# Hybrid trunk on one core: token-tile scalar multiplications on GpSimd, low parts of the output weights on VectorE, and no branch at a layer's end

## What is computed

```python
for l in range(DEPTH):                                   # DEPTH = 2, SEQ = 512, D_MODEL = 1024
    sh_m, sc_m, g_m, sh_f, sc_f, g_f = split(c_act @ ada_w[l] + ada_b[l], 6)
    hm = rms_norm(x, norm_mix_g[l]) * (1.0 + sc_m) + sh_m
    z, xbc, dt_raw, cq, ckv, krope, mq, mk, mv = split(hm @ w_in[l])
    y_ssd = ssd_mixer(z, xbc, dt_raw, ...)
    y_mla = rms_norm(mla_mixer(cq, ckv, krope, ...), mla_out_g[l])
    y_moba = rms_norm(moba_mixer(mq, mk, mv, ..., rel_bias), moba_out_g[l])
    y = concatenate([y_ssd, y_mla, y_moba]) @ w_out[l]
    x = x + g_m * y
    hf = rms_norm(x, norm_ffn_g[l]) * (1.0 + sc_f) + sh_f
    x = x + g_f * moe_ffn(hf, ...)                       # top 2 of 16 experts, one group
```

## Time and profile before

| | before |
|---|---|
| median of 3 executions | 1483.41 us (1477.52 to 1484.29) |
| the profiled execution | 1484.28 us, its span 1482.5 us |
| mean granted TensorE clock | 0.949 of full speed |
| PE busy | 1331.1 us, 90% of the span |
| DVE busy | 1165.1 us, 79% |
| ACT busy | 735.0 us, 50% |
| POOL busy | 257.7 us, 17%, in 300 instructions |

### The profile page before, as it was taken

One profiled execution on the slowest core, in us unless ns is written; L12 is line 12 of the kernel. 1 busy time (PEld: TensorE's weight loads), 2 busy tenths in 40 slices (PEclk: granted clock), 3 DMA queues, 4 the chain that ended last, 5 costly groups with the idle time before them and its releaser, 6 DMA issues. The chain is left out here.

```text
span 1482.5 us, 17406 instructions
## 1 busy us (share of the span) xinstructions
PE 1331.1 (90%) x6467; PEld 1050.8 (71%) x6467; DVE 1165.1 (79%) x1372; ACT 735.0 (50%) x967; POOL 257.7 (17%) x300
## 2 busy tenths in 40 slices
PE   6799987869989999999949998886898999999994
PEld 3677865657878888888647777564677788888882
DVE  3669856894679999999855987398657899999985
ACT  1334343562337777777413342345413777777760
POOL 0100135461011000000120012339001110010002
PEclk9899997989999999999969999898899999999997
DMA  9676521423579999998548573133327899999955
GB/s 361 234 263 225 191 92 56 142 88 141 211 285 365 413 401 416 410 407 351 210 164 301 172 256 118 57 114 114 128 99 284 336 399 410 404 415 403 410 186 185
DMA packets 95461, 378.64 MB, mean 255 GB/s; under 512 B 5961, under 2 KB 8759, under 8 KB 85768
## 3 DMA queue, kind: packets, MB, share of 16 engines
q1 hardware_dynamic: 71816, 307.83, 54.7%
q0 software_dynamic: 15232, 55.63, 9.6%
q10 hardware_dynamic: 8320, 13.96, 2.7%
HBM read 344.58 MB, written 32.82 MB: 255 GB/s over the span
## 5 line engine op out<-in xcount | busy, mean ns | idle before, releaser
L1278 PE MATMUL ps<-mod_rounded,work_rounded 128*128 128x512 f32 x340 | 136.9, 403 | 1.1 <-DVE work_rounded L2284 1.1
L1280 PE MATMUL ps<-mod_rounded,work_rounded 128*128 128x512 f32 x340 | 134.6, 396 | 0.0
L1739 DVE SCALAR_TENSOR_TENSOR gain<-ring,csil,gain 128x512 f32<-128x512 f32 x134 | 111.6, 833 | 3.3
L1279 PE MATMUL ps<-ring_rounded,work_rounded 128*128 128x512 f32 x288 | 113.9, 396 | 0.0
L2143 DVE TENSOR_TENSOR ring_rounded<-ring,mod_rounded 128x2048 fp32r<-128x2048 f32 (+1 forms) x54 | 102.9, 1930 | 1.4
L1279 PE MATMUL ps<-work_rounded 128*128 128x512 f32 x256 | 101.0, 395 | 0.0
L2143 DVE TENSOR_TENSOR work_rounded<-work,mod_rounded 128x2048 fp32r<-128x2048 f32 (+1 forms) x48 | 91.3, 1931 | 9.9 <-ACT mod_rounded L1638 8.7
L2527 POOL DMA_INDIRECT work<-ffn_rows,slot_idx x34 | 42.0, 1236 | 302.8 <-PE ps L1264 270.1
L929 PE MATMUL ps<-ring_rounded,actT_rounded 128*128 128x512 f32 (+1 forms) x256 | 93.9, 367 | 0.0
L1638 ACT ACTIVATE mod_rounded<-ring 128x2048 fp32r<-128x2048 f32 (+1 forms) x54 | 85.9, 1625 | 0.0
L929 PE MATMUL ps<-work_rounded,mod_rounded 128*128 128x512 f32 (+1 forms) x192 | 77.1, 401 | 4.0 <-ACT work L1405 4.0
(11 more groups left out here) (371 smaller groups left out, 3647.2 us busy)
## 6 DMA issues: line engine op xcount, KB each, us to landing
ring<-in_ada_w SPq DMA_DIRECT2D x38, 1024.0 KB, 5.3
ring<-in_moe_w_gate SPq DMA_DIRECT2D x18, 2048.0 KB, 10.0
ring<-in_moe_w_up SPq DMA_DIRECT2D x18, 2048.0 KB, 10.4
ring<-in_moe_w_down SPq DMA_DIRECT2D x18, 2048.0 KB
work<-in_moe_w_up SPq DMA_DIRECT2D x16, 2048.0 KB, 10.7
work<-in_moe_w_down SPq DMA_DIRECT2D x16, 2048.0 KB, 11.6
work<-in_moe_w_gate SPq DMA_DIRECT2D x16, 2048.0 KB, 10.2
expert_rows<-work POOLq DMA_DIRECT2D x32, 512.0 KB, 7.9
```

What stands on the lines that cost most here:

```text
L1278: pe.matmul(ps[j][:, :], xl, hi, start=k == 0, stop=False)
L1279: pe.matmul(ps[j][:, :], xh, lo, start=False, stop=False)
L1280: mm = pe.matmul(ps[j][:, :], xh, hi, start=False, stop=k == KD - 1)
L1739: add(v.scalar_tensor_tensor(acc, w, csil[:, k:k + 1], acc, ALU.mult, ALU.add))
```

## The change

Four edits:

1. `times_rstd` on GpSimd is a loop over the four token tiles, each a `tensor_scalar` by the column of 1/rms, where it was one `tensor_tensor` with the column broadcast.
2. GpSimd no longer makes low parts of the output weights. VectorE makes (0, 1) at n = 25 and (1, 0) right before its wait on `yrs`. PE counts one semaphore instead of two.
3. The Ifs on `L < DEPTH - 1` are gone, so each layer, the last too, loads, rounds and subtracts for a next one.
4. PE's eight `by_token` products and VectorE's eight adds stand behind the Ifs on `nov > 1` instead of ahead of them (with the bodies rewritten to match).

```diff
@@ sync
-                with sp.If(L < DEPTH - 1):
-                    load_first_in(sp, (L + 1) % DEPTH)
-                    sp.dma_start(mod[:, 0:2 * D], mod_rows[bass.ds(L + 1, 1), 0:2 * D].broadcast_to([P, 2 * D])
-                                 ).then_inc(next_b, 16)
-                    sp.wait_ge(y_ps, 2 * (NTL - 1))
-                    load_mix_gain(sp, (L + 1) % DEPTH)
-                    sp.wait_ge(next_b, 16)
+                load_first_in(sp, (L + 1) % DEPTH)
+                sp.dma_start(mod[:, 0:2 * D], mod_rows[bass.ds(L + 1, 1), 0:2 * D].broadcast_to([P, 2 * D])
+                             ).then_inc(next_b, 16)
+                sp.wait_ge(y_ps, 2 * (NTL - 1))
+                load_mix_gain(sp, (L + 1) % DEPTH)
+                sp.wait_ge(next_b, 16)
@@ tensor, out_products
-                            pe.wait_ge(*OUT_LOW[2 * b + k // 4])
+                            pe.wait_ge(out_w_lo, 2 * b + k // 4 + 1)
@@ scalar
-                with a.If(L < DEPTH - 1):
-                    a.wait_ge(y_ps, 2 * (NTL - 1))
-                    first_in_hi(a)
+                a.wait_ge(y_ps, 2 * (NTL - 1))
+                first_in_hi(a)
@@ vector
-                    if n == 19:
-                        out_weights_lo(0, 0)
+                    if n in (19, 25):
+                        out_weights_lo(0, (n - 19) // 6)
...
                 for q in range(8 * T - 3 - FIRST_Y, Y_EARLY):
                     y_low(q)
+                out_weights_lo(1, 0)
                 v.wait_ge(yrs, 3)
...
-                with v.If(L < DEPTH - 1):
-                    last_out(True)
-                with v.If(L > DEPTH - 2):
-                    last_out(False)
+                e = NTL - 1
+                first_in_lo(v, 0, 2 * (len(IN_ORDER) - 1))
+                y_out(e, e % 2, halves=(0,))
+                first_in_lo(v, 1, 2 * (len(IN_ORDER) - 1))
+                y_out(e, e % 2, halves=(1,))
+                v.wait_ge(next_b, 16)
+                mix_gain(v)
@@ gpsimd
                 def times_rstd(dst, src, rstd_, n):
-                    return g.tensor_tensor(dst, src, rstd_.to_broadcast([P, T, n]), ALU.mult)
+                    for t in range(T):
+                        ins = g.tensor_scalar(dst[:, t, :], src[:, t, :], rstd_[:, t, :], None, ALU.mult)
+                    return ins
...
-                for b, half in ((0, 1), (1, 0)):
-                    g.wait_ge(out_w_hi, 2 * b + half + 1)
-                    raw, lo, hi = out_part(b, half)
-                    g.tensor_tensor(lo, raw, hi.bitcast(F32), ALU.subtract).then_inc(out_w_lo_g, 1)
```

More of the change, by code:

```diff
@@ L409, in trunk @@
     out_w_lo = sem("w_out_low_done")
-    out_w_lo_g = sem("w_out_low_done_by_gpsimd")
     hf_wr = sem("ffn_rows_stored")
@@ L1189, in _ @@
                 pv(8 * T - 1)
-                OUT_LOW = [(out_w_lo, 1), (out_w_lo_g, 1), (out_w_lo_g, 2), (out_w_lo, 2)]
                 def out_products(b, t, ks, opens=False, closes=False):
@@ L1330, in by_token @@
                                      start=True, stop=True)
[L1332 to L1335, removed]
                 with pe.If(nov > 1):
+                    pe.wait_ge(y_ev, 2 * NTL)
                     with pe.Fori(0, NOV - 1) as i:
                         with pe.If(nov > i + 1):
+                            for b in range(2):
+                                for t in range(T):
+                                    by_token(b, t).then_inc(cb_ps, 1)
                             pe.wait_ge(ov_x, i + 1)
@@ L1365, in _ @@
                             pe.wait_ge(ov_ye, i + 1)
-                            for b in range(2):
-                                for t in range(T):
-                                    by_token(b, t).then_inc(cb_ps, 1)
+                for b in range(2):
+                    pe.wait_ge(y_ev, 2 * (NTL - 1) + b + 1)
+                    for t in range(T):
+                        by_token(b, t).then_inc(cb_ps, 1)
             @block.scalar
@@ L2327, in add_by_token @@
                     return v.scalar_tensor_tensor(x_, ps[2 * t + b][:, :], over_w[:, t, n:n + 1], x_, ALU.mult, ALU.add)
[L2329 to L2344, removed]
                 hidden(NTL - 1)
@@ L2359, in _ @@
                         with v.If(nov > n):
+                            for b in range(2):
+                                for t in range(T):
+                                    v.wait_ge(cb_ps, 2 * T * (n - 1) + T * b + t + 1)
+                                    ins = add_by_token(n - 1, b, t)
+                            ins.then_inc(ov_x, 1)
                             v.wait_ge(ov_si, n)
@@ L2363, in _ @@
                             slot_tokens(n)
+                            v.wait_ge(ov_x, n)
+                            v.tensor_copy(over_w[:, :, 0:1], over_w[:, :, n:n + 1])
                             v.wait_ge(ov_yp, n)
@@ L2366, in _ @@
                             v.tensor_tensor(ysb[:, 0, 512:1024], ps[7][:, :], gf[:, 512:1024], ALU.mult).then_inc(ov_ye, 1)
[L2367 to L2371, removed]
+                            v.wait_ge(cb_ps, 2 * T * (n + 1))
+                for b in range(2):
+                    for t in range(T):
+                        v.wait_ge(cb_ps, T * b + t + 1)
+                        add_by_token(0, b, t)
             @block.gpsimd
```

## The result

The changed kernel takes 1516.06 us in the median of 4 executions (1515.55 to 1517.7), the kernel before 1483.85 (1477.52 to 1485.46) beside it: a ratio of 1.0226, 95% interval 1.0202 to 1.0250. It is slower. The forecast was 1512 us, range 1482 to 1530. The profiled execution has a span of 1513.9 us at a mean granted clock of 0.933, where before had 1482.5 and 0.949.

A forecast was written before the change was run, and what follows sets the result against it. PE, busy 90%, was taken to wait in attention for GpSimd's staging and a held VectorE instruction. From 1484.3, staging +35.8, low parts -11.0 and layer end +4.05 gave 1513.1, less 0.9 for the median: 1512 us, range 1482 to 1530.

The forecast's parts named there:

- Staging, +35.8: GpSimd's 20 staging instructions per layer become 80; longer stages that PE waits for add 17.9 us per layer, 35.8 in all.
- most of 0.924 is fixed: GpSimd's scalar multiply, 0.924 us for 128x256, is mostly fixed cost, so 32, 64, 96 elements take 0.57, 0.62, 0.67.
- each microsecond moves the rest by one: In five or six of eight staging stages, each microsecond of longer staging moves the rest of the layer.
- rival B: Dearer staging (+46) and PE's clock falling after longer waits, 4 to 8 us: 1527 to 1531 us, chance 0.15.
- the slack of the first stage: First head's staging has about 1.7 us to spare, so of 3.5 us growth only 1.8 reaches the path.
- 4.5 against 4.0 of slack: Fifth staging stage grows 4.5 us against 4.0 to spare, PE starting later, so it adds 0.
- The low parts, -11.0: VectorE's held instructions run normally, -15.6 us; its added subtractions cost 4.6 in all; net -11.0.
- the wait of 2.95: VectorE's 2.95 us wait at 339.69 for a GpSimd chain, expected to hide the half (1, 0) subtraction at no cost.
- Rival C: Low parts give nothing back, since VectorE's chain after step 25 stays as long: 1524 us, chance 0.10.
- The layer's end, +4.05: Without the branch, the last layer's end, last store to GpSimd's drain end, takes 24.15 us like layer 0, not 20.1.
- The branches and moved order, 0: Dropped branches, and PE's eight products and VectorE's eight adds moved across an If, cost nothing beside other work.
- Rival A: Small scalar staging instructions are cheap, below about 0.40 us for 128x64, so not slower: 1481 us, chance 0.17.

## Why the prediction was right, and where it was not

The time (1512 against 1516.06) and the direction were right, and the mechanism too: the small instructions lengthen stages that PE waits for. That it came so near is partly luck, since two steps of the staging sum were wrong and nearly made up for each other. Point by point, with the spans of single edits:

- **Staging, +35.8.** Measured alone: 40.2 by the medians, 34.6 by the profiled executions; beside the other parts 40.8 and 46.0. So the sum is near or low, by which of these one takes, and two of its steps were wrong in opposite directions. The step "most of 0.924 is fixed", from which 0.57, 0.62 and 0.67 us came, failed: it is 0.36, 0.44 and 0.53, since TENSOR_SCALAR by a column costs 2.6 ns an element and not the 1.57 of the form with two streams. So a MoBA stage grew by 2.1 (the first two by 2.8; forecast 3.5) and an MLA stage by 3.2 to 4.1 (forecast 4.5). And the step "each microsecond moves the rest by one" left out the clock: I had put it in rival B alone, as 4 to 8 us. It was 3 us from head 3 to 4 and 4.1 from 4 to 5 in each layer of the changed kernel, 14 in all. The first interval went the other way: 21.7 and 23.5 us before, 19.1 and 19.0 after, -7 in all. Part of that is the slack of the first stage, which starts the count 2.9 us later; part is the clock of the one execution of before that was profiled, 0.84 and 0.78 in this interval, for the changed kernel with the old staging takes 19.0 there at 1.00. Against that kernel the first interval gives nothing back, and this is much of why staging comes to 46.0 there.
- **Stage by stage.** The fifth, with "4.5 against 4.0 of slack" and 0, was right as a stage (17.2 with the MLA stages alone, 17.0 before) and wrong as an interval (20.4), by the clock. The sixth was 3.2 and not 4.5, plus 4.1 of clock. For the seventh the forecast was 3.2 and the interval grew by 4.1 and 2.3, which holds clock as well (before it was 10.7 us at 1.00 and 12.5 at 0.73, after 14.8 at 0.63); for the eighth 2.9, measured 1.3 and 1.0.
- **The low parts, -11.0.** Measured alone: -12.2 by the medians, -10.5 by the spans. VectorE's held instructions are back at 0.48 and 1.53, the wait of 2.95 is 1.21, so the half (1, 0) did hide in it, and the row at 328.83 shows the half (0, 1) among the softmax work. No run has its 2.28 us per layer apart, so only the net of -11.0 is confirmed. Rival C, at 0.10, is refuted by this run. One of the rows isn't of the kind that the forecast names: the instruction at 311.41 reads one tile and a column of scalars, not two inputs, and it was held all the same, 4.51 us for 0.48.
- **The layer's end, +4.05.** Measured 4.4 in the changed kernel and 4.9 alone, from last store to barrier; 6.7 by the medians, interval 0.24% to 0.64%. The reason was right, in a finer form: 3.6 from loads that make the last store land later and the gathers start later, and 1.3 in gathers that run beside VectorE's subtractions.
- **The branches and moved order, 0.** No difference that can be told.
- **Rival A** fails on its price: it needed less than 0.40 us for 128x64, and 0.44 came. It was close.
- **Rival B** had the right term and the wrong price for it: the clock cost some 14 us in its four places for the 4 to 8 that it gave, while its instructions of 0.65 to 0.73 us did not come.
- **The price per element.** By the line of 2.6 ns with a fixed 0.28, what the Trainium skill says of one-input operations at near line rate (GPSIMD Engine Reference, "Engine selection") doesn't hold for this form: the 128x256 took 0.92 where the two-input form of the same size took 0.62.

What stays open is what sets PE's clock in an interval. The runs show that it can change with the stages ahead (from 3 to 4 it is 17.2 us with the MLA stages longer and 20.2 with the MoBA ones), but it was low there too with the waits for the third and fourth stage gone (19.9), and one kernel had 17.4 in one layer and 20.9 in the other. They show that it can be 0.92 or 0.50 for the same instructions (12.4 against 16.5), and that a filler ahead of one wait moves it elsewhere. They don't show a rule by which one could have said beforehand 14 us.

## What to carry to other kernels

An engine at 17% of the span can be the bound, when its short steps stand right ahead of the busiest engine's: price a rewrite there by where each step is waited for, and look first whether the step can simply be issued earlier, where the engine is idle. That move was worth 13 to 14.5 us here, as much as the good part of the change, and it hid the scalar form's whole cost between the heads whose stages were moved (8 us), though not what the clock cost behind them. When such a wait grows, count the clock that PE comes out with as a term of its own, and read busy time for a fixed number of matmuls, since that separates the clock from the waiting. On GpSimd, replacing one instruction over four tiles by four smaller ones pays the fixed part of 0.28 us four times, and a form with fewer inputs isn't cheaper for that.

## What was not expected of the hardware

- GpSimd's TENSOR_SCALAR by a column of scalars took 362, 442 and 526 ns (medians) for 32, 64 and 96 elements and 923 for 256. The TENSOR_TENSOR with the same column broadcast took 622 for 256. The form with fewer streams is the slower one per element.
- The same 48 matmuls, in kernels whose instructions at this place are the same, ran at 0.92 in one execution's layer 0 and at 0.50 in its layer 1: 12.4 us against 16.5. So the clock makes steps of 4 us within one execution.
- Filling a wait of PE with transposes brought the clock behind that wait back (0.62 us instead of 1.06 for four transposes), in one kernel for over 10 us and in the other for 1 us, and it was low again two heads later at the latest.
- The clock fell to 0.50 between heads 3 and 4 also where PE had had no wait over 1.5 us since head 1 (19.9 us at 0.85).
- A store of 512 KB landed 2.9 us after its issue, and 6.2 us after it with 3.5 MB of loads under way, and GpSimd's gathers stood behind it.
